# Tuning a two-block transformer kernel: first weights in halves, attention's results turned inside attention, three banks for side jobs

## The reference

```python
for l in range(2):                                   # first block
    h = rmsnorm(x, g_mix_pre[l])
    mk, mv = split(rmsnorm(mem, g_mem[l]) @ w_mem_kv[l])
    if l == 0: main, mq = mlstm_mixer(h, w_in_a, ...)         # 4 heads
    else:      main, mq = swa_mixer(h, w_in_b, sinks, k_sh, v_sh)  # 12 heads, window 128
    mix = concat([main, memory_attention(mq, mk, mv)]) @ w_out[l]  # 4 memory heads
    x = x + rmsnorm(mix, g_mix_post[l])
    x = x + rmsnorm(swiglu(rmsnorm(x, g_ffn_pre[l]), w_ffn_in[l], w_ffn_out[l]), g_ffn_post[l])
    if l == 0: k_sh, v_sh = shared_kv(x, g_kv, w_kv)
# second block: layer A, a convolution of 31 taps with gates and memory attention;
#               layer B, top-128 sparse attention with gates and memory attention
#               each: x = layer_norm(4**0.25 * x + y @ w_out, g, b)
```

## Time and profile before

| | us |
|---|---|
| median of 3 runs (2065.64 to 2070.49) | 2070.37 |
| profiled execution, its own time | 2071.07 |
| its span, first to last instruction | 2069.6 |

### The profile page before, as it was taken

The page is one execution under the profiler, slowest core; times in us unless marked ns, Lnnn a source line. Parts: engine busy times, 40 slices in busy tenths (PEclk is TensorE's granted clock), DMA queues, the critical chain, the costliest instruction groups (busy, mean ns, idle before and its releaser), DMA issues.

```text
span 2069.6 us, 25481 instructions
## 1 busy us (share of the span) xinstructions
PE 2007.2 (97%) x10032; PEld 1671.1 (81%) x10032; DVE 1178.9 (57%) x2622; ACT 928.5 (45%) x1926; POOL 229.5 (11%) x185
## 2 busy tenths in 40 slices
PE   7999999999999999999999999999999999999998
PEld 7987788888887877788888888887867887788887
DVE  4526553443235677564344225998986537878744
ACT  5547453443124467454344123357745133356731
POOL 1001010000001000010000001576750100000000
PEclk9999999999999999999999999999999999999999
DMA  5421123222233222222322232222231332211131
GB/s 203 157 82 42 41 92 102 100 85 100 102 102 112 102 72 97 79 92 99 102 102 84 99 114 91 102 82 82 82 112 62 107 117 82 82 44 39 42 122 61
DMA packets 29511, 190.07 MB, mean 92 GB/s; under 512 B 3456, under 2 KB 3728, under 8 KB 8144
## 3 DMA queue, kind: packets, MB, share of 16 engines
q1 hardware_dynamic: 25696, 175.98, 24.8%
q0 software_dynamic: 2544, 10.37, 1.5%
q10 hardware_dynamic: 1152, 2.10, 0.3%
HBM read 184.24 MB, written 4.19 MB: 91 GB/s over the span
## 4 chain that ended last, share of the span: by engine, by line
PE 82%; DVE 12%; ACT 5%; issue 1%; DMA 0%; SPq 0%; DVEq 0%; ACTq 0%
PE bank L432 24%; PE bank L434 23%; PE bank L433 23%; DVE bank L2251 5%; PE bank L1913 1%; PE bank L1901 1%; PE bank L588 1%; ACT WH L375 1%; PE bank L1293 1%; DVE WL L399 1%; PE bank L1906 1%; PE bank L1800 1%; PE bank L1278 1%; DVE WL L404 1%; PE bank L1391 1%
## 5 line engine op out<-in xcount | busy, mean ns | idle before, releaser
L432 PE MATMUL bank<-XH,WH 128*128 128x512 f32 (+2 forms) x1504 | 586.3, 390 | 7.8 <-DVE WL L399 3.8
L434 PE MATMUL bank<-XH,WL 128*128 128x512 f32 (+2 forms) x1504 | 560.0, 372 | 0.0
L433 PE MATMUL bank<-XL,WH 128*128 128x512 f32 (+2 forms) x1504 | 559.7, 372 | 0.0
L432 PEld LDWEIGHTS bank<-XH,WH 128*128 128x128 f32 (+1 forms) x1504 | 282.0, 187 | 68.3 <-issue 13.7
L433 PEld LDWEIGHTS bank<-XL,WH 128*128 128x128 f32 (+1 forms) x1504 | 282.1, 188 | 53.0 <-issue 5.5
L434 PEld LDWEIGHTS bank<-XH,WL 128*128 128x128 f32 (+1 forms) x1504 | 281.8, 187 | 50.2
L404 DVE TENSOR_TENSOR WL<-RAW,WH 128x2048 fp32r<-128x2048 f32 x60 | 137.5, 2292 | 285.0 <-ACT WH L378 284.9
L378 ACT ACTIVATE WH<-RAW 128x2048 fp32r<-128x2048 f32 x81 | 154.8, 1911 | 265.4 <-PE bank L434 265.4
L399 DVE SCALAR_TENSOR_TENSOR WL<-RAW,cols,WH 128x256 fp32r<-128x256 f32 (+2 forms) x456 | 201.6, 512 | 82.3 <-ACT WH L375 82.2
L375 ACT ACTIVATE WH<-RAW,cols 128x256 fp32r<-128x256 f32 (+2 forms) x456 | 200.8, 522 | 43.0 <-PE bank L434 35.5
L2251 DVE SCALAR_TENSOR_TENSOR bank<-conv_in,cols,bank 128x512 f32<-128x512 f32 x290 | 198.1, 748 | 1.1
(11 more groups left out here) (324 smaller groups left out, 3102.5 us busy)
## 6 DMA issues: line engine op xcount, KB each, us to landing
RAW<-weights SPq DMA_DIRECT2D x164, 1024.0 KB, 4.8
row_a<-rows POOLq DMA_DIRECT2D x6, 512.0 KB, 5.0
x_res<-x SPq DMA_DIRECT2D x4, 512.0 KB, 10.8
kv<-mem_park POOLq DMA_DIRECT2D x2, 1024.0 KB, 5.7
out<-x_res ACTq DMA_DIRECT2D x8, 256.0 KB, 2.1
mem_tok<-mem SPq DMA_DIRECT2D x1, 1024.0 KB, 7.0
mem_tok<-mem POOLq DMA_DIRECT2D x1, 1024.0 KB, 5.1
mem_park<-m_keys POOLq DMA_DIRECT2D x2, 512.0 KB, 2.9
```

The lines of the kernel that those rows point to most:

```text
L432: pe.matmul(ps, ah, bh, start=first, stop=False)
L433: pe.matmul(ps, ah, bl, start=False, stop=False)
L434: return pe.matmul(ps, al, bh, start=False, stop=last)
```

## The change

1. **Start.** The loads are issued in the order constants, x's first quarter, gains, first half of unit 0 (`A_CHUNK` is 428 columns), second half, x's second quarter, unit 1, the rest. ACT and DVE make the parts of tiles 0 and 1 before they split unit 0. PE multiplies tiles 0 and 1 with blocks 0 and 1, turns tiles 2 and 3, then multiplies with blocks 2 and 3.
2. **Layer 0's attention.** The four blocks of (tile 0, half 1) of `w_out` move from `LATE_TILE` into steps 29 to 32.
3. **Shared keys.** `in_b_pe` takes all four tiles with unit 0, then all four with unit 1. Tiles 2 and 3 are turned two tiles of product earlier. In the tail that precedes it, DVE makes the parts of tiles 2 and 3 before it lowers the second unit.
4. **Layer 1's attention.** `mixed` is turned by tile and half inside the steps (`SLIDE_TURNS`: steps 30, 34, 42, 46, 54, 58, 66, 70). 16 blocks of the product with `w_out` stand behind the 136 entries beside it. The loop has 73 steps, and from step 62 the ring is `five` (banks 3 to 7). S and T move to other memory. After it stand four tiles instead of eight.
5. **End of layer 1.** The first unit of layer A is split and lowered in quarters in the tail.
6. **Layer A.** The units from the third on use a ring of three banks (0 to 2), the memory jobs one of three (3, 6, 7) instead of two. The third split of `a_out` moves from behind the loop to its step 11.

```diff
-        sp.dma_start(cols[:, GC_MIXPRE[0]:N_COLS], cols_in[:, GC_MIXPRE[0]:N_COLS]).then_inc(*loaded_first.mark("first", by=16))
-        for j in range(2):
-            sp.dma_start(RAW[j][:, :], weights_in[j]).then_inc(*raw[j].mark("unit", j, by=16))
-            for pair in range(2):
-                load_x(j, pair)
+        load_x(0, 0)
+        sp.dma_start(cols[:, GC_MIXPRE[0]:N_COLS], cols_in[:, GC_MIXPRE[0]:N_COLS]).then_inc(*gains_there.mark("gains", by=16))
+        sp.dma_start(RAW[0][:, 0:2 * A_CHUNK], weights_in[0, :, 0:2 * A_CHUNK]).then_inc(*raw_first.mark("first_half", by=16))
+        sp.dma_start(RAW[0][:, 2 * A_CHUNK:], weights_in[0, :, 2 * A_CHUNK:]).then_inc(*raw[0].mark("unit", 0, by=16))
+        load_x(0, 1)
+        sp.dma_start(RAW[1][:, :], weights_in[1]).then_inc(*raw[1].mark("unit", 1, by=16))
...
     def in_a_pe():
-        first_tiles_pe(0, 0)
-        first_product_pe(0, 0)
-        first_tiles_pe(0, 1)
-        for t in (1, 2):
-            first_product_pe(t, 0)
+        first_tiles_pe(0, 0)
+        for blocks in ((0, 1), (2, 3)):
+            for t in range(2):
+                first_blocks_pe(t, blocks)
+            if blocks[0] == 0:
+                first_tiles_pe(0, 1)
+        first_product_pe(2, 0)
...
-        (25, "out", 1, 0), (33, "out", 2, 0)) for q in range(4)}
+        (25, "out", 1, 0), (29, "out", 0, 1), (33, "out", 2, 0)) for q in range(4)}
...
     def tail_dve(name, group, mixes, pre, rooted=False):
...
+        for t in range(2, NT if rooted else 2):
+            parts_of_tile_dve(name, t)
         lower_dve([lambda t=t: x_sum_dve(name, t) for t in range(2, NT if pre else 2)])
...
     def in_b_pe():
         PE.wait_ge("split_lo", U["kv", 0] + 1)
+        for first in range(0, NT, 2):
+            for t in range(first, first + 2):
+                if first:
+                    turn_normed_pe(N2, t, False)
+            for t in range(first, first + 2):
+                PE.wait_ge(*after("emptied", *N2, t, 1))
+                kv_tile_pe(t, 0)
         PE.wait_ge("split_lo", U["kv", 1] + 1)
+        for t in range(NT):
             kv_tile_pe(t, 1)
...
+    OUT_BLOCKS = {len(BESIDE) + 4 * n + q: (t, b, q) for n, (t, b) in enumerate(((0, 0), (2, 0), (1, 0), (0, 1)))
+                  for q in range(4)}
-    BESIDE_ENTRIES = max(QUARTERS) + 1
+    BESIDE_ENTRIES = len(BESIDE) + len(OUT_BLOCKS)
+    FIVE_FROM = 62
+    SLIDE_STEPS = len(SLIDE_ORDER) + 1 + BESIDE_LAGS[1]
+    SLIDE_TURNS = {5 + 16 + SH * t + last + 2: (t, half) for t in range(NT) for half, last in enumerate((7, SH - 1))}
...
+            if n in SLIDE_TURNS:
+                t, half = SLIDE_TURNS[n]
+                PE.wait_ge(*after("emptied", "swa_out", SH * t + (SH - 1 if half else 7)))
+                PE.wait_ge(*after("emptied", "mem_out", 1, 4 * t + 3))
+                turn_tile_pe(("mixed", 1), mixed, t, ring, [half])
...
-    LATE_TILE = [(0, 1), (1, 1), (3, 0), (2, 1), (3, 1)]
+    LATE_TILE = [(1, 1), (3, 0), (2, 1), (3, 1)]
...
-        feature_step_pe(k, A_FIRST + s)
+        feature_step_pe(k, A_FIRST + s, ring="three")
...
-            if step in (5, 7):
+            if step in (5, 7, 11):
                 split_act()
```

More of the change, by code:

```diff
@@ L328, in take_bank @@
     def take_bank(ring, *group):
-        first, count = {"product": (0, 4), "spare": (4, 4), "all": (0, 8), "beside": (0, 2), "six": (2, 6), "five": (3, 5), "third": (2, 1), "fourth": (3, 1), "jobs": (6, 2), "sums": (7, 1)}[ring]
-        b = first + turn.get(ring, 0) % count
+        banks = {"product": range(4), "spare": range(4, 8), "six": range(2, 8), "five": range(3, 8), "beside": range(2),
+                 "third": (2,), "fourth": (3,), "sums": (7,), "three": range(3), "jobs": (3, 6, 7)}[ring]
+        b = banks[turn.get(ring, 0) % len(banks)]
         turn[ring] = turn.get(ring, 0) + 1
@@ L1016, in first_tiles_act @@
         act.activation(small[:, 92:93], small[:, 240:241], AF.Copy).then_inc(*A.mark())
-        ACT.wait_ge(*after("first"))
+        for t in range(2):
+            parts_of_tile_act(("n0",), t, halves=[0])
+        ACT.wait_ge(*after("gains"))
         split_act()
-        for t in range(NT):
+        for t in range(2, NT):
             parts_of_tile_act(("n0",), t, halves=[0])
@@ L1055, in first_tiles_dve @@
     def first_tiles_dve():
[L1056 to L1060 removed]
+        for t in range(2):
+            parts_of_tile_dve(("n0",), t, halves=[0])
+        DVE.wait_ge(*after("gains"))
+        lower_dve()
+        for t in range(2, NT):
+            parts_of_tile_dve(("n0",), t, halves=[0])
+        lower_dve()
+        for t in range(NT):
+            parts_of_tile_dve(("n0",), t, halves=[1])
     def in_a_dve():
@@ L1838, in sliding_act @@
                 beside_act(other)
+            if n in SLIDE_TURNS:
+                t, half = SLIDE_TURNS[n]
+                parts_of_tile_act(("mixed", 1), t, halves=[half])
     def sliding_dve():
-        for n, step in enumerate(SLIDE_ORDER):
-            for stage, i in step:
+        for n in range(SLIDE_STEPS):
+            for stage, i in SLIDE_ORDER[n] if n < len(SLIDE_ORDER) else []:
                 if i < 16:
```

176 lines of the change are left out of this document (84 added, 92 removed).

## The result

The changed kernel takes 2046.64 us (median of 4 runs, 2045.82 to 2046.79), the kernel before 2068.01 in the same comparison (4 runs, 2065.48 to 2070.49): a ratio of 0.9898, interval 0.9886 to 0.9911. The prediction was 2056.0, between 2049.5 and 2063. The profiled execution took 2046.61 at a span of 2045.2, 24.46 us less than that of the kernel before.

The account below looks back on a forecast made before the run. PE was taken as the bound, busy 2007.2 of 2069.6 us, so gains come only from its waits and slow clock. Seven terms summed to 14.75, taken from the profiled 2071.07: 2056.3, stated as 2056, range 2049.5 to 2063.

Parts of the forecast that it names:

- 1 start: Kernel start: earlier loads and tile parts bring the first product forward; 0.7 us gained, between -0.5 and 1.8.
- 2 fill, layer 0: Layer 0's attention, steps 29 to 32: four blocks moved into PE's idle time; 2.2 us gained, between 0 and 2.7.
- 3 shared keys: Shared keys: wait shrinks from 2.15 to 0.8 and the clock's fall goes; 3.05 us gained, between 0 and 3.9.
- 4 attention, layer 1: Layer 1's attention: 7.5 saved at best, less 3.6 for turned halves and 0.9 for late quarters; 3.0, between -1 and 6.5.
- 5 tail: Tail of layer 1: lowering in quarters is done earlier; 0.6 us gained, between 0 and 2.3, no clock gain counted.
- 6 layer A: Layer A: third job bank saves 7.4, less a new 2.2 wait and 1.4 for exps; 3.8, between -2.2 and 5.2.
- 7 `a_out`: `a_out`: splitting three steps earlier removes PE's 1.43 us wait for a lowered unit; 1.4 gained, between 0.8 and 1.5.
- The rival of the faster loads: Start: x's quarter and the half unit not slowed by later loads, PE 3 us earlier; 2054.0 us, chance 0.03.
- The rival in which attention hides nothing: Both layers' attention: DVE and ACT bound every step, so both attention gains are 0; 2061.5 us, chance 0.18.
- more of it is filled: Attention layer 1 gains 5.5, layer 0 2.7, layer A 4.8, one more clock fall gone (1.7); 2050.6 us, chance 0.15.

Follow-up runs that it names:

- e1: Kernel before with the new start alone (load order, first unit in halves, parts of tiles 0 and 1 first): 2063.80 us against 2066.16.
- e2: Kernel before with the new start alone, but x's first quarter issued behind both halves of unit 0: 2068.92 us, ratio 1.0013.
- e5: Kernel before with only the four w_out blocks moved into steps 29 to 32 of layer 0's attention: 2063.01 us against 2067.35.
- e3: Kernel before with the shared keys' part of the change alone: 2062.79 us, ratio 0.9985.
- e4: Changed kernel with layer A's four product banks kept up to slot 7 and three banks from slot 8 on: 2044.54 us.
- e6: Kernel before with layer 1's attention changed alone: 2062.36 us, ratio 0.9977.
- e9: Changed kernel with layer A's banks as before (four for products, 6 and 7 for jobs): 2051.16 us.
- e14: Changed kernel itself run again, unchanged, for a second profile: 2045.63 us.
- e11: Changed kernel with only DVE's subtraction made twice for six turned halves in layer 1's attention: 2048.82 us.
- e15: Kernel before itself run again, unchanged, for a second profile: 2065.93 us.
- e12: Changed kernel plus three banks from slot 8, reordered tail, PE waiting per lowered block at the start, and unit 0's first half issued from ACT's queue: 2041.60 us.
- e7: Changed kernel with both ACT's copy and DVE's subtraction made twice for six turned halves in layer 1's attention: 2049.75 us.
- e13: Changed kernel plus three banks from slot 8, reordered tail, and PE waiting per lowered block at the start, loads left alone: 2040.48 us.

## Why the prediction missed, step by step

In the two profiled executions 24.46 us lie between the kernels, and 14.75 were forecast:

| term | forecast | measured | of it clock | shown by |
|---|---|---|---|---|
| 1 start | 0.7 | 2.8 (3.3 in e1) | start's own | e1, e2 |
| 2 fill, layer 0 | 2.2 | 2.0 | | e5, e3, e4 |
| 3 shared keys | 3.05 | 3.1 | 1.7 | e3 |
| 4 attention, layer 1 | 3.0 | 4.4 | | e6, e2, e3 |
| 5 tail | 0.6 | 0.9 | | matching with e5, e6 |
| 6 layer A | 3.8 | 3.8 | | e9 with e14, e11 |
| 7 `a_out` | 1.4 | 1.7 | | matching |
| sum | 14.75 | 18.7 | | |
| other falls, six to two | 0 | 5.8 | all | e14, e15 |

**The base of the sum** is the step that failed worst. I wrote that the sum is made against 2071.07 and that I don't correct for the 0.70 above the median. Correcting the 0.70 would not have been enough: the median of three was itself near the upper end. The profile had seven falls of the clock, and I treated the six that I gave no term as a part of the work that stays. They don't: e15, the same kernel, has four of the seven no more. Taken from 2066.6, the median of 77, the forecast sum would have given 2051.9, and the measured one 2047.9, 1.3 above the result. So of the 9.4 us between forecast and result 4.5 are the base and 4.0 the terms, nearly all of it terms 1 and 4.

**Term 1** is the largest miss among the terms, and its failing step is the landing of the first loads. I read 70 GB/s over the first 5 us as what the queues can move, and so put the landing of x's first quarter at 8 to 8.5 and that of the half unit at 9.5. They landed at 5.4 and 7.8. The rate went with that order of loads: the changed kernel, with x first, moves 158 in the same window, and e2, with the halves of the unit ahead of x, 88:

```profile
0.00:5.00 5.00, 0.00 (x0) 0.00 (x0) 0.00 (x0) 1.49 (x2) 1.09 (x8) 1.00 0.64 158
...
0.00:5.00 5.00, 0.00 (x0) 0.00 (x0) 0.00 (x0) 1.49 (x2) 1.10 (x8) 1.00 0.67 88
```

It was not that too little had been asked for: in the kernel before the whole of unit 0 is issued at 1.63. Why the unit's first bytes come slowly and x's don't is not shown.

The rival of the faster loads had the mechanism (3 us, not slowed by what is queued behind) and 0.03 of the chance. What is paid for is what stands ahead (e2: a megabyte, 4.4 us later than in the changed kernel) and what is issued at once beside it (e12: 1.2 later). With over 2 MB queued behind it x's quarter still lands 4.3 us after its issue; no run leaves that out. An estimate by the figures of the Trainium skill (DMA: Bandwidth & Descriptors, "Anatomy of one DMA") had the landing at 4.4; measured were 5.4, nearer than my 8. The size of the term is not sharp: against the kernel before's first profile the nine profiles with this start are 2.7 to 3.9 ahead at 55, and the kernel before's own second profile is 1.0 ahead there.

**Terms 2, 3, 5 and 7** hold, 3 in both its parts: the wait became 0.70 (forecast 0.8) and the fall went. In the ten us of steps 29 to 32 PE issues 55 matmuls (42 before, about 54 forecast). Term 7 is 0.2 above its upper bound of 1.5, and nothing here says why.

**Term 4** had the right sign and bounds. Its price for the turned halves was nearly right (3.6 forecast, 3.1 measured), for another reason than mine: I took it as DVE's time, the busiest link, and it is about PE's own time for the transposes, while one pair on ACT and DVE is hidden and only a second would cost 0.77 (e7). The part that failed is the 0.9 for quarters lowered late, which didn't come: behind step 61 7.5 us of work were saved, all that I had counted as the best case (with the fall 8.6), and PE has no gap in the 27.3 us there. 7.5 less 3.1 is the 4.4. (A quarter of 5.53 is 1.4 and not the 1.1 of my sum, so that the best case should have been 7.2.) The rival in which attention hides nothing is refuted. 4.4 lies between the forecast's 3.0 and the 5.5 of "more of it is filled", which also had one more fall gone.

**Term 6** came as written, the wait for the gated product at the start of the fourth unit (2.13, forecast 2.2), once:

```profile
1291.23 0.68 DVE L2269 TENSOR_TENSOR conv_in<-row_b,bank 128x512 f32<-128x512 f32 x1
1291.97 0.55 PE L438 MATMUL bank<-XH,WH 128*128 128x512 f32 x1 [2.13 <-DVE conv_in L2269]
```

The gain behind it was 6.2, above the 5.3 that I took as the limit of DVE. DVE's busy time in the stretch fell from 52.0 to 47.6. Its operations are as long as they were (a tap of the convolution 748 and 746 ns, e9 and changed kernel), but 59 taps lie in the stretch and not 65: the same 238 matmuls are no longer tied to the same share of the convolution, which my limit took for granted. What I hadn't priced is that the new wait can bring a fall of the clock (in three of the five profiles with this wait, none in the twelve without): 3.8 of work became 2.2 in this execution. The 1.4 that I left for exps that ACT makes late was right in size (7.4 became 6.2) and not in its reason: PE shows no gap in this stretch, so that part is luck.

**The start's clock.** From the first product to matmul 228 the changed kernel takes 42.3, its second profile 41.5 and e13 40.9, with the same products. That is the spread of 1 us which the prediction's first term left open. The Trainium skill (TensorE: Matmul & The Clock Gate, "Part 1: The HAM clock gate") says that the count of slow matmuls at the start varies from run to run; these traces agree (8 at full spacing of the lower clock in e4, 12 in the changed kernel), and show falls that vary in the same way far from the start.

**Does seven against two belong to the change?** In part. At four places an edit removes the wait or the idle steps in front of a fall, at one it brings a wait. Over all seventeen profiles, each place in the time of the kernel before:

| place | in front of it before | falls, part not changed | falls, part changed |
|---|---|---|---|
| 232.5 | the idle steps that the fill uses | 4 of 6 | 0 of 11 |
| 655.8 | wait of 2.15 | 6 of 6 | 0 of 11 |
| 843.5 | turning of `mixed` | 3 of 6 | 0 of 11 |
| 1266.8 | wait of 2.44 | 5 of 7 | 0 of 10 |
| 1313 (1292 in the changed kernel) | nothing; the new wait of 2.1 | 0 of 12 | 3 of 5 |

So the edits also lower the chance of falls, and the new wait of the third bank seems to raise it; except at the shared keys the counts are small. Weighted by these shares, the four places other than the shared keys are worth 1.7 us on average (an estimate: 0.67 x 1.65 + 0.5 x 1.08 + 0.71 x 1.48 - 0.6 x 1.65). 2066.6 - 18.7 - 1.7 is 2046.2, and the two medians of the changed kernel are 2046.64 and 2045.63. In the two executions of the table of terms 2.6 of the 5.8 lie at these places; the other 3.2 are the draw of one execution.

**What stays open.** Of the other falls (85.8, 208.6, 287.1, the one near 900, and one between 1381 and 1415 in four profiles) the runs show no cause in the change. At 285.8 and 905.0 PE waits 1.9 us in fourteen profiles, and 7 and 4 of them fall there. 85.8 has no wait just ahead. It fell in exactly those six profiles in which PE's matmuls reached the full rate 2.9 to 3.7 us after the first product, and in none of the eleven in which that took 4.0 to 4.5. How the clock came up at the start thus goes with what it does much later in the same execution; why, no run here shows.

## What to carry to other kernels

Before a sum is made against a profiled execution, count the falls of the granted clock in it and see where its time stands in the spread of many runs; give each fall that follows a removed wait to that edit, and take the others as a range, not as a constant. A low transfer rate in the first microseconds holds for that order of loads and not for another: what counts for the first tile is what is queued ahead of it. An attention step in which DVE is free for a quarter of its time took one more pair of short operations on ACT and DVE (1.29 us) for nothing and charged 0.77 for the second, so the cheapest measurement of such a cover is to do the added work twice. When two traces are matched by the number of an instruction, added instructions count as progress: inside such a stretch compare its length and its counts.

## What the runs showed of the hardware

- The kernel before spreads over 5.7 to 9.5 us on one chip and from 2061.69 to 2071.65 over four, by the number and places of falls to the lower clock. A fall lasts 3.4 us and costs 1.1 to 1.7 (one in e5, at 834.2, lasts 6.8 and costs 1.9).
- In the stretch with the memory jobs, where PE waits for a bank, two falls cost nothing in the end: 1.2 behind and level again at 1419 in e9 (1381.3) and in e15 (1398.4). Two that came behind the last of these waits (e2 at 1415.3, e5 at 1411.1) cost 1.6 each.
- All six profiles with the wait of 2.15 at the shared keys fall there, none of eleven with 0.70. At other waits of 1.9 to 2.1 it is a matter of the execution.
- 512 KB land 4.3 us after issue behind 128 KB, and let PE start 9.9 us after the start of the span behind 1.17 MB (e2).
